# One chunk's norm and first query product moved out of the last mixer and in among the second layer's gathers

## What is computed

```python
def peer_ffn(x, wq, sub_keys, u, v):            # the expert lookup, twice
    ...
        u_sel = jnp.take(u, eidx, axis=0)
        a = jax.nn.gelu(jnp.einsum('chkd,cd->chk', u_sel, xc), approximate=False)
        w = (g * a).astype(x.dtype)
        v_sel = jnp.take(v, eidx, axis=0)
        return jnp.einsum('chk,chkd->cd', w, v_sel)
h = layer_norm(DEEPNORM_ALPHA * h + ffn, ln2_g[l], ln2_b[l])     # end of a layer
# the second block's mixer begins: RMS norm, gain and shift, product with w_in_2
def _rmsnorm(t, g):
    y = tf * lax.rsqrt(jnp.mean(tf * tf, axis=-1, keepdims=True) + EPS)
```

## Time and profile before

| | |
|---|---|
| median of 3 runs | 2771.13 us (2769.49 to 2804.34) |
| the profiled execution | 2770.47 us, of which the span is 2768.7 us |
| busy, share of the span | PE 78%, PE weight loads 40%, DVE 55%, ACT 33%, POOL 27% |
| chain that ended last | PE 43%, DVE 24%, DMA 22%, ACT 6%, issue 3%, POOL 1% |
| HBM read | 893.82 MB, 325 GB/s over the span |
| granted TensorE clock | 0.873 of full speed on average |

### The profile page before, as it was taken

One profiled execution on the slowest core, in us unless ns is written; L12 is line 12 of the kernel. 1 busy time (PEld: TensorE's weight loads), 2 busy tenths in 40 slices (PEclk: granted clock), 3 DMA queues, 4 the chain that ended last, 5 costly groups with the idle time before them and its releaser, 6 DMA issues.

```text
span 2768.7 us, 34398 instructions
## 1 busy us (share of the span) xinstructions
PE 2157.2 (78%) x12180; PEld 1120.5 (40%) x12180; DVE 1529.8 (55%) x3269; ACT 900.3 (33%) x2472; POOL 743.0 (27%) x675
## 2 busy tenths in 40 slices
PE   6886777767568686786877768599978879989887
PEld 3542332222012253253434434377876443333332
DVE  5357848578546548866879755546565432212222
ACT  2226333433333324434555554423221111111111
POOL 1113334334334213334554535111111010000000
PEclk9988878777768887888988889899989889999999
DMA  7687999999999727999999899803102299999994
GB/s 306 239 357 273 419 422 401 421 364 372 421 421 416 278 92 296 351 421 398 421 407 414 358 421 403 355 31 107 62 31 99 88 364 412 420 420 420 420 419 186
DMA packets 122694, 894.60 MB, mean 323 GB/s; under 512 B 16400, under 2 KB 16912, under 8 KB 21776
## 3 DMA queue, kind: packets, MB, share of 16 engines
q0 software_dynamic: 77760, 545.30, 48.4%
q1 hardware_dynamic: 44752, 347.01, 30.8%
HBM read 893.82 MB, written 4.72 MB: 325 GB/s over the span
## 4 chain that ended last, share of the span: by engine, by line
PE 43%; DVE 24%; DMA 22%; ACT 6%; issue 3%; POOL 1%; SPq 0%; DVEq 0%; ACTq 0%; POOLq 0%
PE ps L155 41%; DMA ring<-in_peer_uv,idx_u 15%; DVE ring L1640 6%; ACT arena L125 4%; DMA ring<-in_w_gu 4%; DVE arena L76 4%; DVE arena L1640 2%; PE ps L158 2%; DVE iu L113 2%; DVE arena L109 2%; DMA arena<-in_peer_uv,idx_u 1%; DMA arena<-in_w_gu 1%; DVE ring L76 1%; DVE small L93 1%; DVE arena L89 1%
## 5 line engine op out<-in xcount | busy, mean ns | idle before, releaser
L155 PE MATMUL ps<-ring,arena 64*64 64x512 f32 (+3 forms) x4512 | 835.2, 710 | 310.3 <-ACT arena L125 269.3
L155 PE MATMUL ps<-arena 128*128 128x128 f32 (+8 forms) x3496 | 671.7, 491 | 164.9 <-ACT arena L125 122.1
L1640 DVE CUSTOM_DVE_ANT_0 ring<-ring,h 128x1024 f32<-128x1024 f32 x384 | 481.4, 1254 | 258.3 <-DMA ring<-in_peer_uv,idx_u 225.8
L2926 POOL DMA_INDIRECT ring<-in_peer_uv,idx_u x384 | 427.5, 1113 | 558.4 <-PE ps L155 514.4
L155 PEld LDWEIGHTS ps<-ring,arena 64*64 64x64 f32 (+3 forms) x4512 | 212.6, 148 | 795.2 <-ACT arena L125 526.6
L155 PEld LDWEIGHTS ps<-arena 128*128 128x128 f32 (+4 forms) x3496 | 338.7, 174 | 417.8 <-ACT arena L125 208.7
L125 ACT ACTIVATE arena<-arena 128x1 f32<-128x1 f32 (+1 forms) x1051 | 269.1, 256 | 647.7 <-DVE arena L1640 581.9
L125 ACT ACTIVATE arena<-ps 128x512 f32<-128x512 f32 (+2 forms) x278 | 156.2, 562 | 793.5 <-PE ps L155 708.7
L155 PE MATMUL ps<-ring,hT 128*128 128x512 f32 (+2 forms) x800 | 265.5, 487 | 8.0 <-DVE hT L84 4.4
L76 DVE TENSOR_TENSOR arena<-arena,ps 128x256 f32<-128x256 f32 (+1 forms) x106 | 57.9, 546 | 348.0 <-ACT arena L125 309.2
L1640 DVE CUSTOM_DVE_ANT_0 arena<-arena,h 128x1024 f32<-128x1024 f32 x128 | 159.8, 1249 | 111.1 <-DMA arena<-in_peer_uv,idx_u 101.5
(11 more groups left out here) (129 smaller groups left out, 1662.0 us busy)
## 6 DMA issues: line engine op xcount, KB each, us to landing
ring<-in_w_gu SPq DMA_DIRECT2D x98, 1024.0 KB, 21.8
ring<-in_w_down SPq DMA_DIRECT2D x52, 1024.0 KB, 21.1
ring<-in_peer_wq SPq DMA_DIRECT2D x16, 2048.0 KB, 10.8
arena<-in_w_gu SPq DMA_DIRECT2D x30, 1024.0 KB, 21.3
ring<-in_w_in SPq DMA_DIRECT2D x10, 2048.0 KB, 20.0
ring<-in_w_mod SPq DMA_DIRECT2D x16, 1024.0 KB, 9.3
arena<-in_w_in SPq DMA_DIRECT2D x6, 2048.0 KB, 11.3
ring<-in_w_gates SPq DMA_DIRECT2D x12, 1024.0 KB, 4.9
```

The lines of the kernel that those rows point to most:

```text
L155: return self.e.matmul(o, lhsT, rhs, start=start, stop=stop, skip_group_check=True)
L1640: v.done(v.e.tensor_tensor_reduce(out=row, in0=row, in1=h[:, n // 128, :], scale=1.0, scalar=0.0, op0=ALU.mult, op1=ALU.add, accum_out=aa[ ...
L2926: g.e.indirect_dma_start(out=landing(l, n), out_offset=None, in_=d["peer_uv"], in_offset=bass.IndirectOffsetOnAxis(ap=idx_u[:, n:n + 1], a ...
```

## The change

1. **Chunk 0's norm and turning move into layer 1's lookup** (`AHEAD_AT`). ACT squares chunk 0 after n = 200 (`x_squares`), DVE makes the variance after n = 206 (`x_variance`), POOL takes its power after issuing gather 211, DVE scales the rows after n = 216 (`x_normed`, into `x_ahead`, columns 1024 to 2047 of the arena), PE turns them after the weighted sum of n = 222 in two banks of `OTHERS` (`turned_x`), and DVE and ACT copy them into `hT` after n = 228 (`x_turned`).
2. **Chunk 1 alone** goes through the same steps at the mixer's start.
3. **Rq c = 0** (8 products) stands at the head of PE's list for the mixer, ahead of chunk 1's turning, in a bank among 0 and 1; `rows_mm` for Rq does c = 1 alone, in its old phase. Chunk 1's two banks are taken among all eight.

```diff
+AHEAD_AT = (200, 206, 216, 222, 228)
...
+        x_ahead = ar(1024, 1024)
...
-            def rows_mm(tag, xT, w, n, *ready, nk=8, woff=0, wstride=512, grain=8, among=range(8)):
+            def rows_mm(tag, xT, w, n, *ready, nk=8, woff=0, wstride=512, grain=8, among=range(8), chunks=(0, 1)):
                 yield
-                bs = [fresh(*tag, c, among=among) for c in range(2)]
+                bs = {c: fresh(*tag, c, among=among) for c in chunks}
...
                 for c in range(2):
-                    for k in range(nk):
+                    for k in range(nk if c in chunks else 0):
...
                     weighted_sum(n, two)
+                    if l and n == AHEAD_AT[3]:
+                        turned_x(0, x_ahead, OTHERS)
                     advance(background, beside(l, n))
...
+            def turned_x(c, xn, among=range(8)):
+                for k0 in (0, 4):
+                    b = fresh("hxT", c, k0, among=among)
+                    pe.wait_ge(*at("hx", c))
+                    turn4(b, lambda k: xn[:, k * P:(k + 1) * P], k0, "hxT", c, k0)
...
-                                       among=among)
+                                       among=among, chunks=(1,) if name == "Rq" else (0, 1))
...
             def second():                                  # PE
                 s = x_side
-                xn = s.T(0, 4).rearrange("p (c n) -> p c n", c=2)
-                run(turn_pairs(("hxT",), lambda c, k: xn[:, c, k * P:(k + 1) * P], 8, ("hx", "each")))
+                first_rows = ("ps", s.tag, "Rq", 0)
+                b = fresh(*first_rows[1:], among=(0, 1))
+                pe.wait_ge(*at("loaded", s.tag, "Rq"))
+                for k0 in (0, 4):
+                    pe.wait_ge(*at("out", "hxT", 0, k0))
+                for k in range(8):
+                    t = pe.mm(b[:, :], hT[:, k, 0:P], s.weights(8)[:, k * 512:(k + 1) * 512], k == 0, k == 7)
+                pe.done(t, first_rows)
+                turned_x(1, s.T(2, 2))
...
                     if n in NORM_AT:                       # DVE
                         next(first)
+                    if l and n == AHEAD_AT[1]:
+                        x_variance(0)
+                    if l and n == AHEAD_AT[2]:
+                        x_normed(0, x_ahead)
+                    if l and n == AHEAD_AT[4]:
+                        x_turned(0)
...
             def second():                                  # DVE
-                rms("hx", xn, h, st["ss"], st["rs"])
-                run(turned_affine(hT, ("hxT",), gsx, modT))
+                x_variance(1)
+                x_normed(1, s.T(2, 2))
+                x_turned(1)
...
+                    if l and n == AHEAD_AT[0]:             # ACT
+                        x_squares(0, x_ahead)
+                    if l and n == AHEAD_AT[4]:
+                        x_turned(0)
...
             def second():                                  # ACT
-                rms("hx", xn, h, st["ss"], ("h", 4))
-                run(turned_affine(hT, ("hxT",), gsx, modT))
+                x_squares(1, s.T(2, 2))
+                x_turned(1)
...
+                    if l and n == AHEAD_AT[1] + 5:         # POOL
+                        rsqrt(st["rs"][:, 0:1], ("hx", "var", 0), "hx", "rstd", 0)
...
-                rsqrt_by_chunk(st["rs"], "hx")
+                rsqrt(st["rs"][:, 1:2], ("hx", "var", 1), "hx", "rstd", 1)
```

More of the change, by code:

```diff
@@ L1705, in decays, with x_variance, x_normed, x_turned @@
                 v.ts(dec[:, 4:8], rd[:, 4:8], col, None, ALU.mult, None, ("decay",))
+            def x_variance(c):
+                v.wait_ge(*at("hx", "sq", c))
+                v.ts(st["rs"][:, c:c + 1], st["ss"][:, c:c + 1], 1.0 / D, 1e-6, ALU.mult, ALU.add, ("hx", "var", c))
+            def x_normed(c, xn):
+                v.wait_ge(*at("hx", "rstd", c))
+                v.ts(xn, h[:, c, :], st["rs"][:, c:c + 1], None, ALU.mult, None, ("hx", c))
+            def x_turned(c):
+                v.wait_ge(*at("ps", "hxT", c, 0))
+                for j in range(4):
+                    v.ts(hT[:, j, c * P:(c + 1) * P], tile_of("hxT", c, 0)[:, j * P:(j + 1) * P],
+                         gsx[:, j:j + 1], modT[:, j:j + 1], ALU.mult, ALU.add, ("out", "hxT", c, 0))
             def rms(tag, xn, src, ss, rs, *ready):
@@ L2340, in squares, with x_squares, x_turned @@
                 a.act(scratch, h[:, c, :], ACT.Square, ("sq", s, c), accum_out=st["ss"][:, c:c + 1])
+            def x_squares(c, xn):
+                a.wait_ge(*at("h", 4, c))
+                a.act(xn, h[:, c, :], ACT.Square, ("hx", "sq", c), accum_out=st["ss"][:, c:c + 1])
+            def x_turned(c):
+                a.wait_ge(*at("ps", "hxT", c, 4))
+                for j in range(4):
+                    a.act(hT[:, 4 + j, c * P:(c + 1) * P], tile_of("hxT", c, 4)[:, j * P:(j + 1) * P], ACT.Identity,
+                          ("out", "hxT", c, 4), bias=modT[:, 4 + j:5 + j], scale=gsx[:, 4 + j:5 + j])
             def rms(tag, xn, src, ss, *ready):
```

## The result

Over 20 runs of each, the changed kernel takes 2782.2 us (median) against 2772.1; the ratio is 1.0031, 95% interval 1.0021 to 1.0041. On the 2771.1 us of the first three runs that is +8.6 us (5.8 to 11.4); the plain medians lie 10.1 us apart, within that interval. One of the 20 runs of the changed kernel took 5146.69 us and is not in the ratio. The forecast was +3.7, a time of 2774.8 us. The median lies 1.2 us above the upper end of the range (2781), the time by the ratio (2779.7) inside it, but in the part that the prediction had given to its rival B (2777 to 2784, chance 0.15) and not in its own forecast of +1 to +6. The sign and both waits were right; the sizes were not.

What follows compares the result with a forecast made beforehand. It took the DMA engines to bound the lookup and PE the mixer's start. Lookup +2, way to the first product -2.4, bank wait and cold clock +4.1 gave +3.7 us: 2774.8 us, range 2766 to 2781.

Steps and rivals of the forecast that it cites:

- rival B: Lookup: held banks leave a thin queue that empties twice, costing 8 us instead of 2; 2777 to 2784, chance 0.15.
- both waits: PE waits for held PSUM banks: before dX3 in the lookup, and 9.2 us before Rq c = 1 in the mixer.
- The way to the first product: Mixer's start: Gk's first product starts 1.3 to 2.4 us sooner; gain in all 2.4 us, clock included.
- A warmer clock into Gk: Gk's first 32 instructions: a product just before may keep PE at 2.4 GHz; 0.5 us counted of 1.7.
- The Rq product of chunk 0 costs nothing at its new place: Mixer's start: it fits PE's idle time, done before chunk 1's turns, and takes 7.0 us out of the mixer.
- The bank wait in the mixer: After gab c = 1: PE stands 9.2 us until ACT copies Rq c = 0 out; Rq c = 1 starts 2.4 us later.
- Rival A: Mixer: the bank wait costs nothing, so it gains 9.4 us and the lookup gives back 2; 2763.7, chance 0.15.
- The cold clock behind it: Mixer, after the 9 us of idle time: PE comes out at half speed, costing 1.7 us.
- The lookup, "I take 2 us": Layer 1's lookup: held banks delay dX3 and gather 233, which lands 1 to 2 us late; loss 2 us, bounds 0 and 4.
- gathers 234 and 235 have been issued by then: Lookup: PE's wait for P4's bank, up to some 1716.5, comes after these gathers are issued.
- 3 us before 232 has landed: Lookup: rival B decides if gather 233 is issued later than about 1711 us.
- Rival C: The lookup hides its wait and the clock stays high into Gk; 2771 us, chance 0.18 together with D.

Runs made afterwards that it cites:

- e1: Changed kernel with chunk 1's turned rows put through banks 2 and 3; ratio 0.9994.
- e3: Changed kernel with chunk 0's rows turned through idle banks 0 and 1, copies still after 228; ratio 0.9973.
- e7: e3 plus products that nothing reads, four behind the early product and two behind chunk 1's turns; ratio 0.9956.
- e6: Changed kernel, banks untouched, with ACT copying Rq c = 0 out right after chunk 1's turned rows; ratio 0.9986.
- e2: Changed kernel with chunk 0's turned rows copied out after gather 224 instead of 228; ratio 1.0014.
- e11: Changed kernel with chunk 0's turned rows copied out after 229 instead of 228; ratio 1.0046.
- e5: Changed kernel with chunk 0's turned rows copied out after 226 instead of 228; ratio 1.0004.
- e12: The changed kernel itself timed again, with a profile of its own; ratio 1.0031.

## Why the prediction was half right

- **The way to the first product.** Forecast gain 1.9 us without the clock, measured 2.0. Right; that it fell so near the middle is luck, for in the other versions without filler it is 1.4 to 2.4, by the clock of the last sums and of the turns.
- **A warmer clock into Gk ("I count 0.5 us of it").** Wrong: the first 32 instructions took 9.09 us, not less than the 8.83 of before, and 10.1 in e1 and e3. The row that I had set against it, 8.86 us after only 2.04 us of idle time, was the nearer one. But the low clock does not start at the 2.11 us of idle time ahead of Gk: the turns ahead of them, behind 3.66 us of idle time, already took 1.41 us against 1.06 in e7. With the gaps filled in the same place, e7 ran both at the high clock.
- **The Rq product of chunk 0 costs nothing at its new place.** Right: 8.27 us in PE's idle time, done 3.7 us before the turns.
- **The bank wait in the mixer.** The step that I rested on holds: 9.2 us forecast, 9.22 measured, released by the copy that I had named; e1 and e6 take it away in two ways. Rival A fell with it for this kernel. Its price of 9.4 us for the mixer without the wait came out as 7.0 in e1 and 9.5 in e6: the difference is the clock of the turns and of Gk.
- **The cold clock behind it.** "8.83 - 7.15 = 1.7 us": too small a term. Rq c = 1 took 3.0 us more than at full speed (9.93 to Gq's start against 6.9). The same product behind the same 9.22 us took 1.7 to 1.8 us more than the 7.11 of e1 in e2 and e11 and 3.0 more in the changed kernel, e5 and e12. So 1.7 was the lower end, taken as the value; what decides between the two is not shown. The mixer came to +3.7 instead of +1.7.
- **The lookup, "I take 2 us".** This is the larger miss, 6.2 us, more than the upper bound of 4. Gather 233 itself was nearly as computed: issued 1.1 us before dot product 232 (forecast 2), 2.15 us late (forecast 1 to 2). The step that failed is the next one, "gathers 234 and 235 have been issued by then". They had been issued, with leads of 4.4 and 6.1 us, and were late by another 1.32 and 0.54; and PE, behind by then and partly at half speed, let the lead fall to 3.6 us at gather 238: 1.85 more. I priced one late gather where the lead of the next six was short. Rival B had this mechanism, its second emptying, and a point from which it decides ("3 us before 232 has landed"), which e5 (6.1, free) and e6 (1.8, 6.0 us lost) enclose without fixing it. By my own figures gather 233 was 2 us ahead and so beyond that point; I should have given B's 8 us the weight of the forecast.
- **Rival C** (lookup hides its wait) fell with L = 63.3.
- **The sum.** -2.0 + 0.3 + 2.4 + 3.0 + 6.2 = +9.9 us of the profile, against +3.7.

The Trainium skill's page Perfetto Trace Analysis (Optimizing Tensor Performance, Matmuls), on rotating PSUM banks, is borne out in the mixer by e1, where Rq c = 1 gets another bank and M falls from 58.3 to 47.6 us. But e6 keeps the shared bank, only copies it out sooner, and comes to 45.1: here it was enough that the bank was empty in time.

## What to carry to other kernels

Work moved into a gap is paid for by what it holds, not by its instructions: list each buffer that it takes, who asks for it next, and where in the releasing engine's list the release stands. Where a queue of transfers hides the waits, count the lead of each transfer (from its issue to the use of the one ahead of it) over the next several, not only for the first: here the gathers that followed a first lead of 6.1 us came in time, and those that followed one of 1.8 us did not. And a wait on TensorE costs its length plus the low clock of the product behind it, here 1.7 to 3.0 us behind the same 9.22.

## What was not expected of the hardware

- The product of 32 instructions of 128x256 took 8.59 to 10.16 us in the changed versions without filler, behind 2.11 us of idle time and the turns ahead of it, and 7.14 with the gaps filled; the early product, after the last weighted sum, 7.13 to 9.31 us in different kernels with the same work ahead of it. Products that nothing reads bought 3.8 us of the mixer.
- After the hole the gathers did not come back to their rate of 415 GB/s for some 20 us (289 to 385); from 1739 us on it is 415 and more again.
- The first 1630 us, in which all 14 kernels do the same work, vary by up to 8 us between profiled executions (by 4.9 between two of one kernel), as much as the whole effect; only stretches between marks inside the program could be compared.
